# FFN up projections with the weights stationary, attention outputs scaled after the product, modulation sums at the FFNs' ends

## The chip, the core and the metric

The kernel runs on one core of one Trainium2 chip. The metric is the device time of one execution in microseconds (us). Matmuls run on TensorE (PE; its weight loads are listed as PEld), elementwise work on VectorE (DVE) and ScalarE (ACT), some on GpSimd (POOL); SyncE (SP) starts the weight transfers. Engines run on their own and meet at semaphores. TensorE writes to PSUM, which has eight banks of 512 fp32 columns here: acc0 to acc3, turn0, turn1, score0, score1.

## What is computed

256 tokens of width 1024 go through a block of two layers (unchanged here) and then through this one, of which the reference says:

```
a, g = jnp.split(h @ wi, 2, axis=-1)
return (a * jax.nn.silu(g)) @ wo                       # swiglu; D_FF = 2816
y = 0.5 * swiglu(modulate(x, mod, j), wi, wo)          # half_ffn_sublayer, then layer_norm(ALPHA*x + gate*y)
p = jax.nn.softmax(jnp.concatenate([s_win, s_ctx, sinks], axis=-1), axis=-1)
o = einsum(p[..., :SPAN], v_b) + einsum(p[..., SPAN:], vc)
mod_lat = (silu_c @ mod_w[i] + mod_b[i]).reshape(-1, N_MOD, D_MODEL)
```

Five FFNs run: FFN1 on x, FFN2 on the context, then attention, FFN3 and FFN4 on x, a Fourier mixer, FFN5 on x. Each modulation vector set (layer, j) must be there before the sublayer that uses it.

## The kernel before

**Products.** Every fp32 weight matrix is streamed in pieces of 128x1024. ACT rounds a piece to w_hi, DVE makes w_lo = raw - w_hi (split, L1038 and L1417); four slots hold split pieces, and ACT and DVE are up to four ahead of PE (a slot is free when PE has counted piece_done). Activations are kept the same way (xT_hi, xT_lo; features on partitions). product (L522) issues three fp32r matmuls with the activations stationary (128 features x 128 tokens) and 512 weight columns moving: L524, L525, L526.

**An FFN.** The up projection goes in 11 chunks of 256 hidden features (a and g, so 512 columns). project computes a chunk as two token tiles, 48 matmuls into two banks. ACT takes the silu of the g halves (L1274), DVE multiplies (L1872, hidden). Tokens are then on the partitions, but the down projection needs features there: one chunk later PE transposes hidden with four matmuls (turn_hidden, L842), ACT makes hT_hi (L1278) and DVE hT_lo (L1879). The first chunk stands ahead of a loop of five iterations with two chunks each. After the loop comes the last turn_hidden, and then the down projection: 22 pieces of 12 matmuls into acc0 to acc3. FFN3, FFN4 and FFN5 begin with project_first: the tokens 0 to 127 are turned (turn_tile, L561) and multiplied while the second tile's layer norm still runs. gate_rows (L830) ends the first chunk on PE.

**Modulation.** In four of the FFNs (FFN1 to FFN4) one modulation set of the future is computed on the side: POOL loads mod_w (L440), DVE sums eight scaled rows (mod_feature, L1536), and after each 512 columns PE adds over the partitions with four fp32 matmuls of one column (mod_sum, L632), which the profile lists as eight. That is one mod_sum in each loop iteration and one in the down projection.

**Attention.** Eight iterations u, each with two heads. PE: scores(u+1) (L934), values(u-1) (L963), turn_probs(u) (L947). DVE adds the band and takes maxima (L1972), ACT takes exp (L1322), DVE the inverse sums (L1984). POOL then multiplies the probabilities by them (L477, four instructions of 128x512 in each u), and PE transposes the result through three banks in turn; DVE and ACT move them out (L1989, L1330). ACT and DVE split the value products (L1333, L1996).

## Time and profile before

| what | us |
|---|---|
| median of 3 runs | 1750.22 |
| lowest, highest | 1747.34, 1750.8 |
| profiled execution, its own time | 1747.65 |
| its span, first to last instruction | 1745.9 |
| mean granted TensorE clock | 0.966 |

The profile is of one execution. A busy share says how much of the span an engine had an instruction under way. In the timeline a matmul's length runs past the start of the next one, so what a matmul costs in a stream is the spacing of the starts. A note in brackets is the idle time just before an instruction and what ended it.

### The profile page before, as it was taken

Reading aid. Unit: us, or ns where it says so; the run is one execution under the profiler, and the core shown is the slowest. Engines: PE = TensorE matmul, PEld = TensorE weight load, DVE = VectorE, ACT = ScalarE, POOL = GpSimd, SP = SyncE. Lnnn points to the kernel's source line nnn. Section 1 sums busy time; section 2 is a strip of 40 time slices with the busy share of each in tenths; the row PEclk is TensorE's granted clock in tenths of the full one; section 3 lists DMA queues with packets and bytes.
Section 4 is the critical chain, followed back from the end, with each engine's and each line's share of the span. In section 5 each row is a group of like instructions: output and inputs, shape, how many; then the busy total and the mean of one; then the engine's idle time right before and its main releaser. Section 6 shows DMA issues by size and latency. Waiting matters only on the chain.

```text
span 1745.9 us, 23849 instructions
## 1 busy us (share of the span) xinstructions
PE 1627.5 (93%) x7599; PEld 1313.8 (75%) x7599; DVE 1222.9 (70%) x1919; ACT 811.9 (47%) x1256; POOL 169.9 (10%) x207
## 2 busy tenths in 40 slices
PE   6989989899889999999998788999989998989997
PEld 6877768787778887788877357888778886678876
DVE  6877888787977774777667647777487765375545
ACT  5455445556354453444444545444354443254442
POOL 1100001100001110011000551110011100000000
PEclk9999989999989999999999889999999999999999
DMA  9763549642668875788555006887578863255541
GB/s 318 262 212 113 168 138 330 219 169 97 211 214 263 266 240 190 223 267 262 209 175 193 1 25 218 271 265 256 169 229 261 269 234 125 83 166 178 189 177 64
DMA packets 199330, 345.70 MB, mean 198 GB/s; under 512 B 10853, under 2 KB 127901, under 8 KB 198733
## 3 DMA queue, kind: packets, MB, share of 16 engines
q1 hardware_dynamic: 174668, 252.90, 43.5%
q0 software_dynamic: 24576, 91.73, 16.7%
q8 instruction: 46, 0.75, 0.2%
q14 instruction: 40, 0.32, 0.1%
...
## 4 chain that ended last, share of the span: by engine, by line
PE 83%; DVE 8%; issue 3%; ACT 3%; POOL 2%; DMA 0%; SPq 0%; DVEq 0%; ACTq 0%
PE acc L524 24%; PE acc L526 24%; PE acc L525 24%; POOL att_work L477 2%; DVE w_lo L1417 2%; PE score L632 2%; PE turn L842 1%; PE acc L743 1%; PE acc L995 1%; PE score L723 1%; DVE x L1517 1%; ACT turned L1102 1%; PE score L934 1%; ACT w_hi L1038 1%; PE score L830 1%
## 5 line engine op out<-in xcount | busy, mean ns | idle before, releaser
L1417 DVE TENSOR_TENSOR w_lo<-raw,w_hi 128x1024 fp32r<-128x1024 f32 (+1 forms) x490 | 585.4, 1200 | 309.3 <-ACT w_hi L1038 304.2
L1038 ACT ACTIVATE w_hi<-raw 128x1024 fp32r<-128x1024 f32 (+1 forms) x490 | 507.6, 1041 | 575.2 <-PE acc L526 574.8
L524 PE MATMUL acc<-w_hi,xT_hi 128*128 128x512 f32 (+1 forms) x1456 | 589.1, 405 | 33.2 <-DVE xT_lo L1464 12.4
L526 PE MATMUL acc<-w_hi,xT_lo 128*128 128x512 f32 (+1 forms) x1456 | 574.1, 394 | 0.0
L525 PE MATMUL acc<-w_lo,xT_hi 128*128 128x512 f32 (+1 forms) x1456 | 573.9, 394 | 0.0
L524 PEld LDWEIGHTS acc<-w_hi,xT_hi 128*128 128x128 f32 x1456 | 279.4, 192 | 95.7 <-issue 37.8
L526 PEld LDWEIGHTS acc<-w_hi,xT_lo 128*128 128x128 f32 x1456 | 278.6, 191 | 58.9
L525 PEld LDWEIGHTS acc<-w_lo,xT_hi 128*128 128x128 f32 x1456 | 279.9, 192 | 55.3 <-issue 1.2
L440 POOL DMA_DIRECT2D mod_raw<-in_mod_w x144 | 104.3, 724 | 999.1 <-DVE acc_lat L1536 957.7
L1536 DVE SCALAR_TENSOR_TENSOR acc_lat<-mod_raw,silu_c,acc_lat 128x512 f32<-128x512 f32 x252 | 187.8, 745 | 0.9 <-DMA mod_raw<-in_mod_w 0.9
L524 PE MATMUL acc<-w_hi,hT_hi 128*128 128x512 f32 x440 | 174.9, 397 | 0.7 <-DVE hT_lo L1879 0.3
L526 PE MATMUL acc<-w_hi,hT_lo 128*128 128x512 f32 x440 | 173.8, 395 | 0.0
L525 PE MATMUL acc<-w_lo,hT_hi 128*128 128x512 f32 x440 | 173.8, 395 | 0.0
L524 PEld LDWEIGHTS acc<-w_hi,hT_hi 128*128 128x128 f32 x440 | 82.6, 188 | 21.5 <-DVE hT_lo L1879 1.9
L526 PEld LDWEIGHTS acc<-w_hi,hT_lo 128*128 128x128 f32 x440 | 82.6, 188 | 20.0
L525 PEld LDWEIGHTS acc<-w_lo,hT_hi 128*128 128x128 f32 x440 | 82.6, 188 | 19.6
L1274 ACT ACTIVATE silu_g<-acc 128x256 f32<-128x256 f32 x110 | 36.3, 382 | 87.0 <-PE acc L526 87.0
L477 POOL TENSOR_SCALAR att_work<-att_work,att_inv 128x512 f32<-128x512 f32 x32 | 49.6, 1564 | 74.4 <-DVE att_inv L1984 74.4
L1872 DVE TENSOR_TENSOR hidden<-acc,silu_g 128x256 f32<-128x256 f32 x110 | 41.6, 420 | 15.5 <-ACT silu_g L1274 15.5
L1536 DVE SCALAR_TENSOR_TENSOR acc_ctx<-mod_raw,silu_c,acc_ctx 128x512 f32<-128x512 f32 x70 | 52.2, 746 | 0.0
L1879 DVE TENSOR_TENSOR hT_lo<-turn,hT_hi 128x512 f32 (+1 forms) x55 | 38.1, 692 | 9.6 <-ACT hT_hi L1278 3.4
L1179 ACT ACTIVATE work<-score,neg_max 128x256 f32<-128x256 f32 x64 | 29.7, 473 | 28.6 <-DVE neg_max L1637 28.6
...
## 6 DMA issues: line engine op xcount, KB each, us to landing
...
raw<-in_ffn_wo SPq DMA_DIRECT2D x110, 512.0 KB, 4.5
...
```

Source lines behind the costliest of these rows:

```text
L440: pool.dma_start(mod_raw[:, s, :, :], w_mod[l, :, 2 * i:2 * i + 2, at]).then_inc(mod_in[s], 16)
L477: m = nc.gpsimd.tensor_scalar(p, p, att_inv[:, h, t:t + 1], None, ALU.mult)
L524: nc.tensor.matmul(dst, xh, wh, start=start, stop=False)
L525: nc.tensor.matmul(dst, xh, wl, start=False, stop=False)
L526: return nc.tensor.matmul(dst, xl, wh, start=False, stop=stop)
L632: m = nc.tensor.matmul(dst[:, 4 * i + j:4 * i + j + 1], acc[:, 1, j * P:j * P + P], ones[:, 0:1], start=True, stop=True)
L1038: nc.scalar.activation(w_hi[:, i % SPLIT_SLOTS, 0:n], raw[:, s, i % 2 * PIECE:i % 2 * PIECE + n], ACT.Copy).then_inc(hi_ready, 1)
L1274: nc.scalar.activation(silu_g[:, half, t, :], bank[ACC[2 * half + t]][:, FC:2 * FC], ACT.Silu).then_inc(silu_done, 1)
L1417: nc.vector.tensor_tensor(w_lo[:, i % SPLIT_SLOTS, 0:n], raw[:, i // 2 % RAW_SLOTS, i % 2 * PIECE:i % 2 * PIECE + n], w_hi[:, i % SPLIT_SL ...
L1536: m = nc.vector.scalar_tensor_tensor(out=acc[:, 1 if k == KD - 1 else 0, :], in0=w, scalar=by, in1=acc[:, 0, :], op0=ALU.mult, op1=ALU.add)
L1872: nc.vector.tensor_tensor(hidden[:, half, t, :], bank[b][:, 0:FC], silu_g[:, half, t, :], ALU.mult).then_inc(moved[b], 1)
L1879: nc.vector.tensor_tensor(sl(hT_lo), bank[b][:], sl(hT_hi).bitcast(F32), ALU.subtract).then_inc(moved[b], 1)
```

## The change

- **Up projection.** up_product makes the weights stationary (128 x 128 features) and lets xT_hi or xT_lo move, so that hidden features come out on partitions. A chunk is 96 matmuls of 256 tokens; one bank holds a (two feature tiles), the other g. turn_hidden and its transposes go. ACT takes one silu of 512 columns, DVE one product of 512, ACT makes hT_hi from hidden and DVE hT_lo. One of a chunk's four splits now stands behind the silu.
- **First chunk by tile** (up_first: FFN3, FFN4, FFN5): the same matmuls with one token tile each, so 192 matmuls of 128 columns.
- **Down projection.** It starts with the column half 1 of the pieces 0 and 1 (banks acc2, acc3), then their half 0.
- **Modulation sums.** DVE leaves six sums in mod_kept; PE adds them over the partitions after the last down matmul (kept_sums). FFN1 and FFN2 do all 24 fp32 matmuls there; FFN3 and FFN4 do 8 there and 16 behind the next turn_tile. The sets (1,1) and (1,2) change places.
- **Attention.** The probabilities are transposed unscaled. PE spreads the inverse sums over a fifth transposed bank in each u, ACT moves it (move_scale), DVE multiplies the value product by it (scale_out), and POOL splits the result into xT_hi and xT_lo (two instructions of 128x256). The four probability banks and the scale go round the same three banks.

```diff
-            for h in range(AH):
-                pool.wait_ge(inv_ready, h + 1)
-                for t in range(NT):
-                    p = att_probs[:, h // 2 % 2, h % 2, t, :]
-                    m = nc.gpsimd.tensor_scalar(p, p, att_inv[:, h, t:t + 1], None, ALU.mult)
-                m.then_inc(norm_ready, 1)
+            for u in range(AH // 2):
+                pool.wait_ge(out_scaled, u + 1)
+                nc.gpsimd.tensor_copy(xT_hi[:, u, :], att_out[:, u % 2, :]).then_inc(out_hi, 1)
+                pool.wait_ge(out_hi, u + 1)
+                nc.gpsimd.tensor_tensor(xT_lo[:, u, :], att_out[:, u % 2, :], xT_hi[:, u, :].bitcast(F32), ALU.subtract).then_inc(out_split, 1)
...
-            def project_first(banks):
+            def up_first(banks, kept):
                 slots, after = [], [turn_tile(0)]
+                if kept:
+                    kept_sums(KEPT_EARLY, MOD_KEPT)
+                dst = [take(b) for b in banks]
                 for t in range(NT):
-                    dst = take(banks[t])
                     for i in range(4):
                         if t == 0:
                             if i == 2:
...
                         if i % 2 == 0:
                             b, landed_at = after[t][i // 2]
                             pe.wait_ge(moved[b], landed_at)
-                        s = slots[i]
-                        for kk in range(2):
-                            k = 2 * i + kk
-                            m = product(dst[:], xT_hi[:, k, t * P:t * P + P], xT_lo[:, k, t * P:t * P + P],
-                                        w_hi[:, s, kk * 512:kk * 512 + 512], w_lo[:, s, kk * 512:kk * 512 + 512],
-                                        k == 0, k == KD - 1)
+                        for k in (2 * i, 2 * i + 1):
+                            m = up_product(dst, slots[i], k, slice(t * P, t * P + P), t == 0 and k == 0)
...
+            def up_product(dst, s, k, tokens, first):
+                kk = k % 2 * 512
+                for h in range(2):
+                    for j in range(2):
+                        f = slice(kk + h * FC + j * P, kk + h * FC + j * P + P)
+                        d = dst[h][:, j * TOK + tokens.start:j * TOK + tokens.stop]
+                        nc.tensor.matmul(d, w_hi[:, s, f], xT_hi[:, k, tokens], start=first and j == 0, stop=False, skip_group_check=True)
+                        nc.tensor.matmul(d, w_lo[:, s, f], xT_hi[:, k, tokens], start=False, stop=False, skip_group_check=True)
+                        m = nc.tensor.matmul(d, w_hi[:, s, f], xT_lo[:, k, tokens], start=False, stop=k == KD - 1, skip_group_check=True)
...
+            def up_chunk(banks, after=None):
+                dst = [take(b) for b in banks]
+                for i in range(4):
+                    if after:
+                        b, landed_at = after[i]
+                        pe.wait_ge(moved[b], landed_at)
+                    s = piece()
+                    for k in (2 * i, 2 * i + 1):
+                        m = up_product(dst, s, k, slice(0, TOK), k == 0)
+                    m.then_inc(piece_done, 1)
...
+            def kept_sums(first, last):
+                if first == 0:
+                    pe.wait_ge(mod_step, c.next("mod", 8 * MOD_KEPT) + 2 * MOD_RING)
+                    take("score1")
+                for i in range(first, last):
+                    for j in range(4):
+                        m = nc.tensor.matmul(bank["score1"][:, 4 * i + j:4 * i + j + 1], mod_kept[:, i, j * P:j * P + P], ones[:, 0:1],
+                                             start=True, stop=True)
...
-            def ffn(after, mods, then=None):
-                def turn_hidden(half):
-                    landed(*ACC[2 * half:2 * half + 2])
...
-                    dst = take(b)
-                    for f in range(2):
-                        for t in range(NT):
-                            m = nc.tensor.transpose(dst[:, f * TOK + t * P:f * TOK + t * P + P],
-                                                    hidden[:, half, t, f * P:f * P + P], ident[:])
-                    m.then_inc(full[b], 1)
-                    return b
+            def ffn(after, mods, then=None, kept=False, by_tile=True):
                 if after:
-                    project(ACC[0:2], 4, after=after)
+                    up_chunk(ACC[0:2], after)
                 else:
-                    project_first(ACC[0:2])
+                    up_first(ACC[0:2], kept)
                 gate_rows()
...
                 with c.loop(pe, N_FC // 2, per):
-                    project(ACC[2:4], 4)
-                    turn_hidden(0)
-                    project(ACC[0:2], 4)
-                    turn_hidden(1)
-                    if mods:
-                        mod_sum(False)
-                last = turn_hidden(0)
...
+                    up_chunk(ACC[2:4])
+                    up_chunk(ACC[0:2])
+                pe.wait_ge(hidden_split, c.next("hidden", N_FC - 1))
+                dst = [None, None] + [take(b) for b in ACC[2:4]]
...
                         m = product(dst[2 * n + t][:], hT_hi[:, k, t * P:t * P + P], hT_lo[:, k, t * P:t * P + P],
                                     w_hi[:, s, n * 512:n * 512 + 512], w_lo[:, s, n * 512:n * 512 + 512], k == 0, k == KF - 1)
                     return m
-                for k in range(KF - 4):
+                slots = [piece() for _ in range(2)]
+                for k in range(2):
+                    for t in range(NT):
+                        down(k, slots[k], t, (1,))
+                dst[0:2] = [take(b) for b in ACC[0:2]]
+                for k in range(2):
+                    for t in range(NT):
+                        m = down(k, slots[k], t, (0,))
+                    m.then_inc(piece_done, 1)
+                for k in range(2, KF - 4):
                     if k == 4 and then:
                         after = then()
-                    if mods and k == KF // 2:
-                        mod_sum(False)
                     s = piece()
                     for t in range(NT):
                         m = down(k, s, t)
                     m.then_inc(piece_done, 1)
-                pe.wait_ge(moved[last], last_at)
+                pe.wait_ge(hidden_split, c.next("hidden"))
                 slots = []
                 for t in range(NT):
                     for i in range(4):
...
                             m.then_inc(piece_done, 1)
                     if t == 0:
                         m.then_inc(first_done, 1)
+                if mods:
+                    kept_sums(0, KEPT_EARLY if by_tile else MOD_KEPT)
...
-                        pe.wait_ge(norm_ready, c.next("norm"))
+                        pe.wait_ge(exps_ready, c.next("exps"))
...
+                    pe.wait_ge(inv_ready, c.next("inv", 2))
+                    b = att_turn(u, 4)
+                    dst = take(b)
+                    for t in range(NT):
+                        for i in range(2):
+                            m = nc.tensor.matmul(dst[i * AD:i * AD + AD, t * P:t * P + P], att_inv[:, 2 * u + i, t:t + 1].to_broadcast([P, AD]),
+                                                 ident[:], start=True, stop=True)
+                    m.then_inc(full[b], 1)
+                    turned_at[u].append((b, c.now(b) + 1))
...
-            after = ffn(turn_x(), True, turn_ctx_in)
-            after = ffn(after, True, turn_x)
+            after = ffn(turn_x(), True, turn_ctx_in, by_tile=False)
+            after = ffn(after, True, turn_x, by_tile=False)
             attention(after)
             ffn(None, True)
-            ffn(None, True)
+            ffn(None, True, kept=True)
...
-                def chunk(half, n=4):
+                def chunk(half, n=3):
                     split(n)
                     products(4)
-                    for t in range(NT):
-                        nc.scalar.activation(silu_g[:, half, t, :], bank[ACC[2 * half + t]][:, FC:2 * FC], ACT.Silu).then_inc(silu_done, 1)
-                def turn_hidden(k):
-                    src = filled(next_turn())
-                    nc.scalar.activation(hT_hi[:, k, :].rearrange("p k n -> p (k n)"), src[:], ACT.Copy).then_inc(turn_hi, 1)
-                chunk(0, 4 - early)
+                    b = ACC[2 * half + 1]
+                    nc.scalar.activation(silu_g[:], bank[b][:], ACT.Silu).then_inc(moved[b], 1)
+                    split()
+                def hidden_hi(half, k):
+                    act.wait_ge(hidden_ready, c.next("hidden"))
+                    nc.scalar.activation(hT_hi[:, k, :].rearrange("p k n -> p (k n)"), hidden[:], ACT.Copy).then_inc(moved[ACC[2 * half]], 1)
...
+                def move_scale(u):
+                    b = att_turn(u, 4)
+                    nc.scalar.activation(att_scale[:, u % 2, :], filled(b)[:, 0:TOK], ACT.Copy).then_inc(moved[b], 1)
...
+                def chunk(half, features=(), n=3, into=None):
                     for i in range(n):
                         split()
                         if features:
-                            mod_feature(features[i], False)
-                    for t in range(NT):
-                        b = ACC[2 * half + t]
-                        dve.wait_ge(silu_done, c.next("silu_done"))
-                        nc.vector.tensor_tensor(hidden[:, half, t, :], bank[b][:, 0:FC], silu_g[:, half, t, :], ALU.mult).then_inc(moved[b], 1)
-                def turn_hidden(k):
...
-                    c.next(b)
-                    dve.wait_ge(turn_hi, c.next("hi"))
...
-                    nc.vector.tensor_tensor(sl(hT_lo), bank[b][:], sl(hT_hi).bitcast(F32), ALU.subtract).then_inc(moved[b], 1)
-                chunk(0, n=4 - early)
...
+                            mod_feature(features[i], False, into)
+                    a, g = ACC[2 * half:2 * half + 2]
+                    dve.wait_ge(moved[g], c.next(g + " moved") + 1)
+                    nc.vector.tensor_tensor(hidden[:], bank[a][:], silu_g[:], ALU.mult).then_inc(hidden_ready, 1)
+                    split()
+                    if features:
+                        mod_feature(features[n], False, into)
+                def hidden_lo(half, k):
+                    a = ACC[2 * half]
+                    dve.wait_ge(moved[a], c.next(a + " moved") + 1)
...
+                    nc.vector.tensor_tensor(lo, hidden[:], hi.bitcast(F32), ALU.subtract).then_inc(hidden_split, 1)
...
+            def kept_store(l, j):
...
+                nc.vector.tensor_tensor(mod_lat[:, l, at], filled("score1")[:, 0:4 * MOD_KEPT], modb[:, l, at], ALU.add).then_inc(moved["score1"], 1)
...
+                def scale_out(u):
+                    if u > 1:
+                        dve.wait_ge(out_split, u - 1)
+                    nc.vector.tensor_tensor(att_out[:, u % 2, :], filled(ATT_OUT)[:, 0:TOK], att_scale[:, u % 2, :], ALU.mult).then_inc(out_scaled, 1)
...
-            ffn(x, x_ready, mod_lat[:, 0, :], 2, mods=(1, 2), end=by_tile, early=1)
+            ffn(x, x_ready, mod_lat[:, 0, :], 2, mods=(1, 1), end=by_tile, early=1)
```

PE, the end of FFN1's loop body and the start of the down projection; before:

```order
L525 MATMUL acc1<-w_lo,xT_hi 128x512
L526 MATMUL acc1<-w_hi,xT_lo 128x512
L513 REGISTER_ALU
L842 MATMUL turn1<-ident,hidden 128x128 x4
L628 REGISTER_ALU
L507 REGISTER_ALU
L632 MATMUL score1<-ones,acc_lat 128x1 x4
L108 REGISTER_ALU
L108 COMPARE_AND_BRANCH
L842 MATMUL turn0<-ident,hidden 128x128 x4
L524 MATMUL acc0<-w_hi,hT_hi 128x512
L525 MATMUL acc0<-w_lo,hT_hi 128x512
```

The same place after:

```order
L647 MATMUL acc1<-xT_hi,w_hi 128x256
L648 MATMUL acc1<-xT_hi,w_lo 128x256
L649 MATMUL acc1<-xT_lo,w_hi 128x256
L110 REGISTER_ALU
L110 COMPARE_AND_BRANCH
L537 MATMUL acc2<-w_hi,hT_hi 128x512
L538 MATMUL acc2<-w_lo,hT_hi 128x512
L539 MATMUL acc2<-w_hi,hT_lo 128x512
L537 MATMUL acc3<-w_hi,hT_hi 128x512
L538 MATMUL acc3<-w_lo,hT_hi 128x512
L539 MATMUL acc3<-w_hi,hT_lo 128x512
```

The transposes and the sum between the last up matmul and the first down matmul are gone, and the down projection begins in acc2.

PE, the start of FFN3: the first token tile is turned and the first matmuls of the first chunk follow; before:

```order
L561 MATMUL turn0<-ident,x 128x128 x4
L561 MATMUL turn1<-ident,x 128x128 x4
L524 MATMUL acc0<-w_hi,xT_hi 128x512
L525 MATMUL acc0<-w_lo,xT_hi 128x512
L526 MATMUL acc0<-w_hi,xT_lo 128x512
L524 MATMUL acc0<-w_hi,xT_hi 128x512
```

The same place after:

```order
L574 MATMUL turn0<-ident,x 128x128 x4
L574 MATMUL turn1<-ident,x 128x128 x4
L647 MATMUL acc0<-xT_hi,w_hi 128x128
L648 MATMUL acc0<-xT_hi,w_lo 128x128
L649 MATMUL acc0<-xT_lo,w_hi 128x128
L647 MATMUL acc0<-xT_hi,w_hi 128x128
L648 MATMUL acc0<-xT_hi,w_lo 128x128
```

Twelve matmuls of 512 columns for two pieces of one token tile become 48 of 128 columns; the second tile's turn (score0) stands behind them as before.

PE in the attention, from turn_probs(u) to scores(u+2), u = 0; before:

```order
L947 MATMUL turn0<-ident,att_work 128x128 x4
L947 MATMUL turn1<-ident,att_work 128x128 x4
L947 MATMUL acc3<-ident,att_work 128x128 x4
L947 MATMUL turn0<-ident,att_work 128x128 x4
L934 MATMUL score0<-kT,qT 128x512
L934 MATMUL acc0<-kT,qT 128x512
```

The same place after:

```order
L989 MATMUL turn0<-ident,att_work 128x128 x4
L989 MATMUL turn1<-ident,att_work 128x128 x4
L989 MATMUL acc3<-ident,att_work 128x128 x4
L989 MATMUL turn0<-ident,att_work 128x128 x4
L997 MATMUL turn1<-ident,att_inv 64x128 x4
L976 MATMUL score0<-kT,qT 128x512
L976 MATMUL acc0<-kT,qT 128x512
L976 MATMUL score1<-kT,qT 128x512
```

A fifth bank, the spread inverse sums (L997), stands behind the four of the probabilities.

## Rows read from the trace of the kernel before

**Rows 1.** The page: busy time of PE and others, and the chain by engine.

```profile
PE 1627.5 (93%) x7599; PEld 1313.8 (75%) x7599; DVE 1222.9 (70%) x1919; ACT 811.9 (47%) x1256; POOL 169.9 (10%) x207
...
PE 83%; DVE 8%; issue 3%; ACT 3%; POOL 2%; DMA 0%; SPq 0%; DVEq 0%; ACTq 0%
```

**Rows 2.** Windows of one loop iteration, FFN1 (with modulation) and FFN5 (without).

```profile
core 0: us, PE busy (x) PEld busy (x) DVE busy (x) ACT busy (x) POOL busy (x), PEclk, DMA share, GB/s
535.04:558.88 23.84, 23.84 (x114) 19.73 (x113) 17.81 (x24) 10.56 (x16) 3.13 (x5) 1.00 0.83 259
1593.08:1615.77 22.69, 22.69 (x105) 18.80 (x104) 12.70 (x14) 10.56 (x14) 0.00 (x0) 1.00 0.59 185
```

**Rows 3.** Timeline (start us, us, instruction), PE: loop start, first down matmul, FFN1 and FFN5.

```profile
511.02 0.79 PE L524 MATMUL acc<-w_hi,xT_hi 128*128 128x512 f32 x1
...
631.30 0.50 PE L524 MATMUL acc<-w_hi,hT_hi 128*128 128x512 f32 x1
...
1559.05 0.79 PE L524 MATMUL acc<-w_hi,xT_hi 128*128 128x512 f32 x1
...
1674.77 0.50 PE L524 MATMUL acc<-w_hi,hT_hi 128*128 128x512 f32 x1 [0.17 <-DVE hT_lo L1879]
```

**Rows 4.** Timeline, PE: fp32r streams, 23 matmuls of 256 and 43 of 512 columns.

```profile
95.72 0.28 PE L525 MATMUL acc<-w_lo,cT_hi 128*128 128x256 f32 x1
...
98.22 0.28 PE L526 MATMUL acc<-w_hi,cT_lo 128*128 128x256 f32 x1
...
714.35 0.39 PE L526 MATMUL acc<-w_hi,xT_lo 128*128 128x512 f32 x1
...
723.89 0.39 PE L526 MATMUL acc<-w_hi,xT_lo 128*128 128x512 f32 x1
```

**Rows 5.** Fp32 matmuls of 1 column (chain: start, us) and 128 columns (timeline).

```profile
51.60 1.68 PE score L632 x16
...
184.62 2.01 PE L743 MATMUL acc<-wide,work 128*128 128x128 f32 x16
```

**Rows 6.** Timeline, PE: the first chunk of FFN3.

```profile
1065.54 0.77 PE L524 MATMUL acc<-w_hi,xT_hi 128*128 128x512 f32 x1 [2.79 <-DVE xT_lo L1464]
...
1070.37 0.63 PE L526 MATMUL acc<-w_hi,xT_lo 128*128 128x512 f32 x1
1071.38 1.09 PE L561 MATMUL score<-ident,x 128*128 128x128 f32 x8 [0.38 <-DVE x L1517]
...
1080.53 1.88 PE L830 MATMUL score<-gate_diag,ones 128*128 128x512 f32 x4
```

**Rows 7.** Timeline, PE: the first work behind FFN1, FFN2 and FFN3.

```profile
698.92 0.76 PE L524 MATMUL acc<-w_hi,xT_hi 128*128 128x512 f32 x1 [3.11 <-DVE gated L1826]
...
900.68 0.76 PE L524 MATMUL acc<-w_hi,xT_hi 128*128 128x512 f32 x1 [3.11 <-DVE gated L1826]
...
1266.24 1.09 PE L561 MATMUL turn<-ident,x 128*128 128x128 f32 x8 [1.32 <-DVE x L1517]
```

**Rows 8.** Attention: window (columns as Rows 2), and timeline of PE and DVE.

```profile
962.60:1038.10 75.50, 57.18 (x320) 32.70 (x320) 42.60 (x135) 37.71 (x103) 49.60 (x32) 0.86 0.00 1
...
971.02 1.14 PE L947 MATMUL turn<-ident,att_work 128*128 128x128 f32 x8 [2.78 <-POOL att_work L477]
...
979.27 1.08 PE L963 MATMUL acc<-ctx_x,qkv 128*64 128x256 f32 x8
...
984.88 0.69 PE L934 MATMUL score<-kT,qT 64*128 64x512 f32 x1
...
989.44 0.23 DVE L1978 TENSOR_SCALAR att_neg<-att_max,neg_sink 128x2 f32<-128x2 f32 x1
...
1036.28 1.08 PE L963 MATMUL acc<-ctx_x,qkv 128*64 128x256 f32 x8 [0.92 <-ACT ctx_x L1330]
```

**Rows 9.** Groups by line (last numbers: busy us, mean ns), from the page and by form.

```profile
L1417 DVE TENSOR_TENSOR w_lo<-raw,w_hi 128x1024 fp32r<-128x1024 f32 (+1 forms) x490 | 585.4, 1200 | 309.3 <-ACT w_hi L1038 304.2
L1038 ACT ACTIVATE w_hi<-raw 128x1024 fp32r<-128x1024 f32 (+1 forms) x490 | 507.6, 1041 | 575.2 <-PE acc L526 574.8
...
L1989 DVE COPY ctx_x<-turn 128x512 f32<-128x512 f32 x11 | 7.6, 688 | 6.7 <-PE turn L947 6.6
```

151 lines of the change are left out of this document (76 added, 75 removed).

## The prediction, made before the changed kernel was run

> **What bounds the kernel now.** I read the page's busy times and the chain of waits first. PE is busy 93% of the span and is 83% of the chain; DVE is 8% of it [rows 1]. So a change counts by what it takes from or gives to PE's sequence, and off PE only where PE stands and waits. Then I took windows of one FFN loop iteration: PE is busy in all of it, 23.84 us with modulation and 22.69 without, while DVE does 17.81 and ACT 10.56 [rows 2]. The reader is to see that PE never waits in the loop, and that the two windows differ by 1.15 us, the price of one mod_sum in PE's sequence. The timeline of PE at the joints gives the rest: what stands between loop start and first down matmul, how the first chunk by tile runs, how long PE idles behind an FFN, and who holds the attention.
>
> **What a matmul costs.** In a stream, 256 columns of fp32r are spaced (98.22 - 95.72) / 22 = 0.1136 us and 512 columns (723.89 - 714.35) / 42 = 0.2271 us [rows 4]. So 96 matmuls of 256 take 10.9 us and 48 of 512 take 10.9 us: exchanging the operands is free in the loop, and twice as many weight loads still hide behind 256 columns. A full iteration of 96 x 0.2271 = 21.8 us leaves 22.69 - 21.80 = 0.89 us for two turn_hidden.
>
> The Trainium skill speaks against this: "Perfetto Trace Analysis", section "Identifying the Most-Contended Engine", judges TensorE's headroom by the busy share of its weight loads. Taken alone it would double the 18.80 us of an iteration without modulation to 37.6 us, above 21.8, and add some 395 us over the 25 iterations. The 256-column row, where loads already come every 0.1136 us, contradicts that, so I give this no chance.
>
> **Part 1, up loop and start of the down projection.** FFN1 runs from 511.02 to 631.30, 120.3 us, for ten chunks [rows 3]; FFN2, FFN3 and FFN4 are within 0.3 us of that. After: 10 x 10.9 = 109.0 us, plus some 0.2 us that the first matmul behind gate_rows takes longer, 109.2. That is -11.1 us in each of four FFNs, -44.4. FFN5 has no sums: 1674.77 - 1559.05 = 115.7, so -6.5 us. The mod_sum in the middle of the down projection goes in four FFNs: 4 x -1.15 = -4.6 us. Together **-55.5 us**.
> What hides the new hand-over: PE needs acc0 again 12 half products, 2.7 us, after the last up matmul. ACT by then must do silu (not over 1.04 us, a split of 1024 columns), one split (1.04) and hT_hi, DVE one product of 512 columns between them (0.69, as L1989) [rows 9]: 1.04 + 1.04 + 0.6 = 2.7 us, so nearly even; without that cover it would cost up to 1 us per FFN. Behind the silu stands one split on each engine; its piece is needed two pieces (5.4 us) later, so PE doesn't wait for it. DVE has 17.81 of 21.8 us in an iteration, ACT 10.56.
> DMA moves as much in less time: share 0.83 x 23.84 / 21.8 = 0.91, 283 GB/s [rows 2]. I take it as enough; if it isn't, see the third rival.
>
> **Part 2, the first chunk by tile.** This is what the change costs, and the trace has no fp32r matmul under 256 columns. Bounds: nothing beyond the columns (128 at half of 0.1136, 0.057 us, so no loss); and the fp32 rate, where 16 instructions of 128 columns take (2.01 - 0.28) / 15 = 0.115 us each, two to a matmul, 0.23 us [rows 5]. I choose between them by the fp32 matmuls of one column: 16 in 1.68 us, 0.105 us each, though they stream nothing [rows 5]. With one column moving, what is left is the weight load, so I take 0.105 us for any matmul with fresh weights.
> FFN3 today: first matmul 1065.54, the matmuls ahead of the second turn_tile are spaced 0.43 us (half clock: the last of the twelve starts at 1070.37), and the turn waits until 1071.38 for the second tile's layer norm [rows 6]. So 5.8 us of time are there for these two pieces anyway. After: 48 matmuls; 24 in 5.1 us at half clock (0.21 each), 24 at 0.105, 7.6 us: 1.8 late. The other two pieces of the first tile: 48 x 0.105 = 5.0 against 12 x 0.227 = 2.7, 2.3 more. The second tile: 96 x 0.105 = 10.1 against 5.4, 4.7 more. Sum 8.8; three FFNs: **+26 us**.
> The Trainium skill bears on the choice. "TensorE: Matmul & The Clock Gate", section "LDWEIGHTS (loading the stationary operand)", has the load take its columns divided by 1.2 GHz; the row of 0.105 us agrees. The same page, section "Back-to-back issue gap", reports about 81 ns for sustained pairs at 128 columns. By that this part would be an estimated +14 us and the total 12 us lower; no row here shows such a spacing.
>
> **Part 3, the sums at the ends.** 24 fp32 matmuls are 48 instructions, 48 x 0.105 = 5.0 us. Behind FFN1 and FFN2 PE idles 3.1 us for a bank today [rows 7]: +1.9 us each. Behind FFN3 and FFN4 there are 16 instructions, 1.7 us, in an idle time of 1.32: +0.4 each. The remaining 32, 3.4 us, stand behind the turn where PE waits 2.79 or more for xT_lo [rows 6]: +0.5 at most once, since the attention's end has none. Together **+5 us**, from 0 (if the next chunk then starts at full clock; today its first matmuls are spaced 0.43) to +8.
>
> **Part 4, attention.** The stretch of 75.5 us has 49.6 us of POOL in 32 instructions, 1.55 each, 6.2 in every u, at a clock of 0.86 [rows 8]. values(0) starts at 979.27 and values(7) at 1036.28, 8.14 us for each u. Afterwards the first turn_probs need not wait for POOL (idle 2.78 before 971.02), which brings values(0) some 4 us forward. Then what is late next is the ring of three banks: the fourth probability bank of a u takes the first one again, and DVE moves that only after both maxima. From scores (984.88) to the end of those (989.44 + 0.23) are 4.8 us; then scale_out (0.4), a move (0.69, rows 9), the fourth transposes (0.5), the spread sums (8 instructions at 0.115, 0.9): 7.4 us, say 7.5 for each u. 8 x 0.6 = 5 us. Sum **-9 us**; from 0 (no gain if the fifth use of the ring costs what POOL did) to -16 (PE's own work). values(u) also waits for scale_out(u-1), queued on DVE behind two maxima; scores(u+1) cover it. POOL's two instructions of 256 columns in each u (1.6 us by its 1.55 for 512) end before the output product of the fourth piece.
>
> **Sum.** -55.5 + 26 + 5 - 9 = -33.5 us. The profiled execution's own time is 1747.65 (its span 1745.9), so 1714.2; the median lies 2.6 above it: **1716 us**, give or take 9.
>
> **Rivals.**
> - *Narrow fp32r runs at the fp32 rate* (the slower side). At 0.23 us in the three first chunks: 7.8 + 8.4 + 16.7 = 33 us for each instead of 8.8, so 1716 - 26 + 99 = 1789. It decides against the change from 0.16 us on, where the three chunks eat the 33 us. For it: fp32 at 128 columns does cost 0.23. Against: the stream of fp32r halves exactly from 512 to 256 columns [rows 4], with no sign of a second regime. 16%.
> - *Weight loads hide at 128 columns too.* Part 2 is then about 0: 1690. The 0.105 us of the one-column matmuls would be something of fp32 alone. 12%.
> - *Transfers hold the loop.* If more than 259 GB/s doesn't come, an iteration stays at up to 23.84 us in the four FFNs with modulation, 20 x 2.0 = 41 us back at most, 1757; half of it is 1736. DVE would then wait for mod_raw. Against: at a share of 0.83 the engines have room today [rows 2]. 12%.
> - Forecast as summed, 1705 to 1727: 60%.
>
> **How the numbers follow.** The range takes in the forecast, the second rival and the nearer half of the third: 1688 to 1742, which leaves out the fp32 rate (16%) and some 3% beyond the ends. Within 0.2% of before (3.5 us, about what a measurement of this kernel can tell from no change) lies only a corner of the third rival or a milder form of the first: 3%. Slower 16%, faster 81%.
>
> **What would show it.** Loop iteration 21.8 us in FFN1 and FFN5 alike, with no transposes in it (right), or near 23 with waits for mod_raw (third rival). Spacing of the 128-column matmuls in FFN3's first chunk: 0.105, 0.057 or 0.23 us; the stretch from its first matmul to gate_rows 24 us instead of 15. Behind FFN1 the next chunk starts 5 us after the last down matmul instead of 3.1. values(u) spaced 7.5 us, attention about 66 us. I am wrong if the stretch of the first chunks grows by over 15 us, or if PE has idle time inside the loop.

## The result, and the profile after the change

The changed kernel takes 1779.04 us (median of 4 runs, 1776.73 to 1781.66) against 1748.78 us for the kernel before on the same chip (4 runs). The ratio is 1.0176, 95% interval 1.0157 to 1.0195: slower by 1.8%, where 1716 us had been predicted. The profiled execution has a span of 1776.5 us, 30.6 more than before, and it is the one read below.

The page: PE and its weight loads, PE's granted clock in 40 slices, and the chain by engine.

```profile
PE 1688.3 (95%) x10371; PEld 1494.9 (84%) x10371; DVE 1200.4 (68%) x1844; ACT 798.0 (45%) x1201; POOL 129.9 (7%) x191
...
PEclk9999989999989998999998989999899998859999
...
PE 86%; DVE 7%; issue 3%; ACT 2%; DMA 1%; SPq 0%; DVEq 0%; ACTq 0%; POOLq 0%
```

PE is still the bound, busy for 61 us more than in [rows 1]. The second 8 and the 5 near the end of the clock's row belong to a stretch at half clock, 1542.4 to 1590.2 us, that the kernel before didn't have. The windows show it: an up loop iteration of FFN1 and one of FFN5, then the first chunks of FFN3, FFN4 and FFN5, from their first matmul to gate_rows.

```profile
core 0: us, PE busy (x) PEld busy (x) DVE busy (x) ACT busy (x) POOL busy (x), PEclk, DMA share, GB/s
550.00:573.04 23.04, 23.04 (x195) 23.04 (x194) 16.88 (x21) 10.11 (x13) 2.89 (x4) 1.00 0.86 281
1590.43:1613.47 23.04, 23.04 (x195) 23.04 (x194) 9.79 (x10) 8.72 (x10) 0.00 (x0) 1.00 0.52 159
1048.26:1076.72 28.46, 28.46 (x201) 28.46 (x201) 13.19 (x22) 7.51 (x14) 3.98 (x6) 0.77 0.60 199
1263.43:1291.83 28.40, 28.40 (x202) 28.40 (x202) 11.61 (x21) 5.03 (x10) 2.55 (x4) 0.78 0.46 162
1544.27:1586.89 42.62, 42.62 (x201) 42.62 (x201) 13.19 (x22) 7.51 (x14) 1.05 (x2) 0.50 0.31 99
```

Three more windows: the sums behind FFN1, the end of its down projection ahead of them, and the sums behind FFN2:

```profile
690.14:698.07 7.93, 7.93 (x50) 7.93 (x48) 7.86 (x13) 3.47 (x5) 0.00 (x0) 0.65 0.04 7
686.00:690.14 4.14, 4.14 (x19) 3.33 (x18) 2.90 (x8) 3.62 (x6) 0.00 (x0) 1.00 0.05 19
891.98:897.14 5.16, 5.16 (x48) 5.16 (x47) 5.09 (x10) 0.86 (x1) 0.00 (x0) 1.00 0.00 0
```

The first two windows show that an iteration takes 23.04 us with and without modulation (192 x 0.120), and that the weight loads are busy in all of it. The first chunks took 15.0 us before [rows 6]; now they take 28.5, 28.4 and 42.6, and the last ran at a granted clock of 0.50 from end to end although PE never stood still. The joints, in PE's timeline (start us, us, instruction):

```profile
509.87 1.88 PE L881 MATMUL score<-gate_diag,ones 128*128 128x512 f32 x4
...
626.78 0.40 PE L537 MATMUL acc<-w_hi,hT_hi 128*128 128x512 f32 x1
...
690.14 8.07 PE L682 MATMUL score<-ones,mod_kept 128*128 128x1 f32 x48
698.07 0.56 PE L647 MATMUL acc<-xT_hi,w_hi 128*128 128x256 f32 x1
...
959.16 0.66 PE L976 MATMUL score<-kT,qT 64*128 64x512 f32 x1 [0.83 <-issue]
...
1020.92 0.50 PE L537 MATMUL acc<-w_hi,xT_hi 128*128 128x512 f32 x1
...
1060.79 0.41 PE L647 MATMUL acc<-xT_hi,w_hi 128*128 128x128 f32 x1
...
1061.31 0.28 PE L647 MATMUL acc<-xT_hi,w_hi 128*128 128x128 f32 x1
1061.42 0.28 PE L648 MATMUL acc<-xT_hi,w_lo 128*128 128x128 f32 x1
...
1255.27 1.84 PE L682 MATMUL score<-ones,mod_kept 128*128 128x1 f32 x16
1256.98 1.07 PE L574 MATMUL turn<-ident,x 128*128 128x128 f32 x8
1257.88 5.69 PE L682 MATMUL score<-ones,mod_kept 128*128 128x1 f32 x32
1263.43 0.45 PE L647 MATMUL acc<-xT_hi,w_hi 128*128 128x128 f32 x1
```

With these the 30.6 us come apart nearly without rest. The parts are those of the prediction; before and after are PE's own times.

| part | stretch | measured | predicted |
|---|---|---|---|
| 1 | gate_rows to first down matmul, FFN1 to FFN4: 121.6 to 116.9 (FFN4 121.3) | -18.4 | -44.4 |
| 1 | the same in FFN5: 117.0 to 118.6 | +1.6 | -6.5 |
| 1 | first to last down matmul, without mod_sum: 1.0 less in each of FFN1 to FFN4, 0.1 in FFN5 | -4.1 | -4.6 |
| 2 | first chunks: 15.0 to 28.5, 15.0 to 28.4, 15.1 to 42.6 | +54.4 | +26 |
| 3 | sums at the ends (behind FFN1 alone +5.8, FFN2 +2.0, FFN3 and FFN4 +3.1) | +10.9 | +5 |
| 4 | first scores to output projection: 75.5 to 61.8 | -13.7 | -9 |
| | sum | +30.7 | -33.5 |

Parts 1 and 2 miss by 35 and 28 us, part 3 by 6; part 4 was better than said. The four questions for the chip follow from this: what the clock does in the first chunk, why 256 columns cost 0.120 and not 0.1136 us, whether parts 3 and 4 are worth by themselves what the table says, and what is left when only the good parts are kept.

### The profile page after: what moved, and what is told of

It is laid out like the page before. It is cut to its first block, busy times and chain, and to the rows that moved or that the text cites. A ratio compares the mean times of both kernels' runs of the same rounds, so it can differ in the third digit from the quotient of the medians.

```text
span 1776.5 us, 29013 instructions
## 1 busy us (share of the span) xinstructions
PE 1688.3 (95%) x10371; PEld 1494.9 (84%) x10371; DVE 1200.4 (68%) x1844; ACT 798.0 (45%) x1201; POOL 129.9 (7%) x191
## 4 chain that ended last, share of the span: by engine, by line
PE 86%; DVE 7%; issue 3%; ACT 2%; DMA 1%; SPq 0%; DVEq 0%; ACTq 0%; POOLq 0%
PE acc L647 13%; PE acc L649 13%; PE acc L648 13%; PE acc L537 12%; PE acc L539 12%; PE acc L538 12%; DVE w_lo L1465 2%; PE score L682 2%; PE acc L794 1%; PE acc L1045 1%; PE score L976 1%; DMA mod_raw<-in_mod_w 1%; PE score L774 1%; DVE att_work L2025 1%; PE score L881 1%
## 5 line engine op out<-in xcount | busy, mean ns | idle before, releaser
L647 PE MATMUL acc<-xT_hi,w_hi 128*128 128x256 f32 (+1 forms) x1856 | 542.5, 292 | 7.0 <-DVE xT_lo L1512 7.0
L648 PE MATMUL acc<-xT_hi,w_lo 128*128 128x256 f32 (+1 forms) x1856 | 539.5, 291 | 0.0
L649 PE MATMUL acc<-xT_lo,w_hi 128*128 128x256 f32 (+1 forms) x1856 | 539.3, 291 | 0.0
L647 PEld LDWEIGHTS acc<-xT_hi,w_hi 128*128 128x128 f32 x1856 | 372.8, 201 | 9.3 <-issue 9.3
L648 PEld LDWEIGHTS acc<-xT_hi,w_lo 128*128 128x128 f32 x1856 | 372.5, 201 | 1.4 <-issue 1.4
L649 PEld LDWEIGHTS acc<-xT_lo,w_hi 128*128 128x128 f32 x1856 | 372.2, 201 | 0.0
L537 PE MATMUL acc<-w_hi,xT_hi 128*128 128x512 f32 (+1 forms) x576 | 234.6, 407 | 16.0 <-DVE xT_lo L1500 6.9
L538 PE MATMUL acc<-w_lo,xT_hi 128*128 128x512 f32 (+1 forms) x576 | 227.8, 395 | 0.0
L539 PE MATMUL acc<-w_hi,xT_lo 128*128 128x512 f32 (+1 forms) x576 | 227.7, 395 | 0.0
L538 PEld LDWEIGHTS acc<-w_lo,xT_hi 128*128 128x128 f32 x576 | 111.7, 194 | 21.0
```

The costliest lines, as they stand in the source:

```text
L537: nc.tensor.matmul(dst, xh, wh, start=start, stop=False)
L538: nc.tensor.matmul(dst, xh, wl, start=False, stop=False)
L539: return nc.tensor.matmul(dst, xl, wh, start=False, stop=stop)
L647: nc.tensor.matmul(d, w_hi[:, s, f], xT_hi[:, k, tokens], start=first and j == 0, stop=False, skip_group_check=True)
L648: nc.tensor.matmul(d, w_lo[:, s, f], xT_hi[:, k, tokens], start=False, stop=False, skip_group_check=True)
L649: m = nc.tensor.matmul(d, w_hi[:, s, f], xT_lo[:, k, tokens], start=False, stop=k == KD - 1, skip_group_check=True)
```

## The experiments

### The first chunk: width and clock

**wide_first.** The chunk waits for both tiles and runs 96 matmuls of 256 columns.

```diff
-                for t in range(NT):
-                    for i in range(4):
...
-                        for k in (2 * i, 2 * i + 1):
-                            m = up_product(dst, slots[i], k, slice(t * P, t * P + P), t == 0 and k == 0)
+                after.append(turn_tile(1))
+                for i in range(4):
...
+                    for k in (2 * i, 2 * i + 1):
+                        m = up_product(dst, s, k, slice(0, TOK), k == 0)
```

> The changed kernel with one edit: the first chunk of FFN3, FFN4 and FFN5 waits for both token tiles and then runs with 256 columns, 96 matmuls instead of 192 of 128 columns. Theory A (the narrow matmuls are the loss: 0.112 us each at the full clock, 0.213 at the half clock, which they keep): 96 matmuls take 11.5 us at the full clock, up to 20.5 at the half one, after a start 12 to 15 us later. In FFN3 from 1048.3 the first chunk then ends after some 14 + 12 to 20 us = 26 to 34 instead of 28.6; in FFN5 14 + 12 to 20 = 26 to 34 instead of 42.8. Total 1779 - 9 to -16 if the clock rises early, 1763 to 1770. Rival B (the half clock stays through the chunk of FFN5 whatever the width): FFN5 gains 8 us, FFN3 and FFN4 lose 5 each, total 1779 to 1782.

Measured: 1744.82 us (10 runs), ratio to before 0.9985 [0.9968, 1.0001]: 34 us less than the changed kernel, more than either theory gave. The window of its first chunk in FFN3 shows why:

```profile
1054.00:1057.40 3.40, 3.35 (x16) 3.38 (x17) 2.79 (x10) 0.12 (x1) 0.06 (x1) 0.50 1.02 354
1057.60:1067.00 9.40, 9.40 (x80) 9.40 (x80) 2.45 (x2) 2.12 (x2) 0.00 (x0) 1.00 0.82 284
```

With 256 columns the clock came back 3.5 us after the first matmul, in FFN4 after 3.6 and in FFN5 after 3.1 us. I had expected the half clock to last for up to all of the chunk. The narrow chunk held it for 12.9 us in FFN3, 12.8 in FFN4 and 42.6 us in FFN5. So either the narrow stream can't raise the clock, or it lowers it by itself.

**warm_narrow** tells these apart. The narrow chunk stays, and PE is kept busy ahead of it (TN is 448 columns).

```diff
                 dst = [take(b) for b in banks]
+                for _ in range(3):
+                    nc.tensor.matmul(dst[0][:, 0:TN], ident[:], tables[:].rearrange("p t n -> p (t n)")[:, 0:TN], start=True, stop=True)
```

> The changed kernel with one addition: in the idle time between the first turn_tile and the first chunk of FFN3, FFN4 and FFN5, PE runs three fp32 matmuls over 448 columns of a constant, into the bank that the chunk then starts afresh. The narrow first chunk itself stays. In the changed kernel it ran at a granted clock of 0.50 for 13 us in FFN3 and FFN4 and for all of its 43 us in FFN5. Theory A (the stream of narrow matmuls cannot raise the clock, yet keeps what it has): with PE busy ahead of it the chunk of FFN5 runs at the full clock, 192 x 0.112 = 21.5 us instead of 41, and in FFN3 and FFN4 the first half takes 5.4 instead of 10.3 us (then it waits for the second tile, so 0 to 5 us each). Total 1779 - 20 - 0 to 10 = 1749 to 1759. Rival B (the narrow stream lets the clock fall whatever it starts with, or three matmuls are too few): the chunk of FFN5 stays near 43 us, total 1776 to 1783.

Measured: 1748.37 us, 0.9995 [0.9979, 1.0011] of before, 31 us less than the changed kernel. Theory A gave 1749 to 1759, just above it. A window of FFN5, from the second turn_tile to gate_rows:

```profile
1541.95:1558.90 16.95, 16.95 (x152) 16.95 (x153) 7.43 (x15) 5.02 (x10) 1.05 (x2) 1.00 0.47 146
```

The clock is 1.00 in all of it. The same narrow stream keeps the full clock that it is given. From the first turn_tile to gate_rows FFN3 now takes 26.7 us against 32.3 in the changed kernel and 18.9 before. The 7.8 us over before are the cost of the narrow width itself; the rest was the clock. The prediction's 8.8 had 24 matmuls at half clock in it; without them its sum gives 7.0.

**cut_first** asks whether this is a matter of weights being loaded. It is the kernel before with each 512-column matmul of the first chunk cut in four.

```diff
-                            m = product(dst[:], ..., w_hi[:, s, kk * 512:kk * 512 + 512], ...)
+                            for c0 in range(0, 512, P):
+                                m = product(dst[:, c0:c0 + P], ..., w_hi[:, s, kk * 512 + c0:kk * 512 + c0 + P], ...)
```

> The kernel before with one edit: in the first chunk of FFN3, FFN4 and FFN5 each matmul of 512 columns is cut into four of 128, with activations loaded as before; 192 narrow matmuls, as many as in the changed kernel. Theory A (the width alone does it, whatever is loaded): first matmul to gate_rows 28.6 us in FFN3 and FFN4 as in the changed kernel, 20.5 to 43 in FFN5 by when the clock rises: total 1749 + 13.6 + 13.6 + 8 to 28 = 1784 to 1804. Rival B (loading weights instead of activations does it, or the modulation sums ahead of the chunk): the clock rises after some 5 us as before, each chunk costs 8 us more, total 1749 + 24 = 1773.

Measured: 1817.47 us, 1.0399 [1.038, 1.0418]: above even theory A. In FFN3 the clock came back within the chunk as in the changed kernel, in FFN4 and FFN5 not before gate_rows (first turn_tile to gate_rows 32.2, 47.6 and 46.5 us). A window of FFN5's chunk:

```profile
1596.00:1628.00 32.00, 32.00 (x152) 32.00 (x152) 7.58 (x15) 6.08 (x11) 0.00 (x0) 0.50 0.22 73
```

So the width does it, whichever operand is loaded. When the clock comes back varies. PE's second turn_tile in the changed kernel, FFN3 and FFN5:

```profile
1058.53 1.93 PE L574 MATMUL score<-ident,x 128*128 128x128 f32 x8
...
1554.55 1.93 PE L574 MATMUL score<-ident,x 128*128 128x128 f32 x8
```

These eight fp32 instructions interrupt the narrow stream. The clock came back inside a narrow chunk five times in the traces (FFN3 and FFN4 of the changed kernel and of shared_w, FFN3 here), each time 0.4 to 0.7 us behind the end of the second turn_tile. Four chunks with the same turn_tile stayed at the half clock to their end (FFN5 of the changed kernel and of shared_w, FFN4 and FFN5 here). There it came back 3.3 to 3.6 us after gate_rows, of 512 columns, had begun. So no trace shows a return behind narrow fp32r matmuls alone; whether it is turn_tile that brings the clock back was not tested by itself. One run in four of shared_w (below) took 1762 instead of 1777 us at a mean clock of 0.964 instead of 0.955.

### The spacing of 0.120 us in the loops

The prediction took 0.1136 us from 23 matmuls of 256 columns with cT loaded [rows 4]. I went through what differs between these and the loop.

**shared_w** puts the two matmuls with the same weights in a row.

```diff
-  matmul(d, w_hi[:, s, f], xT_hi[:, k, tokens], ...)
-  matmul(d, w_lo[:, s, f], xT_hi[:, k, tokens], ...)
+  matmul(d, w_lo[:, s, f], xT_hi[:, k, tokens], ...)
+  matmul(d, w_hi[:, s, f], xT_hi[:, k, tokens], ...)
   matmul(d, w_hi[:, s, f], xT_lo[:, k, tokens], ...)
```

> The changed kernel with one edit: each group of three matmuls of the up projection runs w_lo.x_hi, w_hi.x_hi, w_hi.x_lo instead of w_hi.x_hi, w_lo.x_hi, w_hi.x_lo, so that the two with the same weights stand in a row. Theory A (the 0.120 us between 256-column matmuls, where the row of before had 0.1136, is there because every matmul has other weights than the one ahead, while in the row of before two of three share them): spacing 0.1136, an iteration of the loop 21.8 us instead of 23.04, total 1779 - 32 = 1747 us. Rival B (a load costs the same whatever stood there): spacing stays 0.120, total 1779 within 3 us.

Measured: 1777.32 us, spacing 0.120. Theory A falls.

**cut_256** exchanges the operands back: the kernel before, with the loop's matmuls cut in two.

```diff
-                            m = product(dst[t][:, 0:n], ...)
+                            for c0 in range(0, n, n // cut):
+                                m = product(dst[t][:, c0:c0 + n // cut], ...)
...
-                    project(ACC[2:4], 4)
+                    project(ACC[2:4], 4, cut=2)
```

> The kernel before with one edit: in the up loop of the FFNs every matmul of 512 columns is cut into two of 256 columns, each with its own load of the activations; as many loads as in the changed kernel, but activations are what stays. Theory A (it is the weights as the loaded side that cost 0.120): spacing 0.1136, iteration without modulation 22.7 us as before, total 1749. Rival B (it is the surroundings, two engines and the transfers busy beside a load every 256 columns, that cost it): spacing 0.120, iteration 22.7 + 1.2 = 23.9, total 1749 + 30 = 1779.

Measured (one run): 1777.9 us, spacing 0.1199. First, second and last of 61 of its matmuls:

```profile
576.77 0.28 PE L526 MATMUL acc<-w_hi,xT_lo 128*128 128x256 f32 x1
576.89 0.28 PE L524 MATMUL acc<-w_hi,xT_hi 128*128 128x256 f32 x1
...
583.96 0.28 PE L526 MATMUL acc<-w_hi,xT_lo 128*128 128x256 f32 x1
```

Which operand is loaded plays no part; with either, halving a matmul costs some 5.5% more per column in the FFNs. FFN5 after the change has a DVE busy 9.8 us an iteration and a DMA share of 0.52, FFN1 16.9 and 0.86, both at exactly 0.120, so the engines beside PE aren't it either.

**wide_six**, **wide_alt** and **wide_bank** change where results go: six in a row to one place; two banks in turn after each matmul; another bank after every three. The lines are shortened.

```diff
wide_six:   for h, j, k in ((h, j, k) for h in range(2) for j in range(2) for k in (2 * i, 2 * i + 1)):
wide_alt:   for j in range(2): for w, xt in ((w_hi, xT_hi), (w_lo, xT_hi), (w_hi, xT_lo)): for h in range(2):
wide_bank:  for j in range(2): for h in range(2):
```

> The kernel with the first chunk of 256 columns (1745 us), with one edit in every chunk of the up projection: the loop over the two features of a piece is the innermost, so that six matmuls in a row add into the same 256 columns of a bank instead of three. Theory A (the 0.120 us in the loops, where the row of before with 256 columns had 0.1136 and six to a place, comes from changing the place of the result every three matmuls): spacing 0.1136, an iteration 21.8 instead of 23.04 us, total 1745 - 31 = 1714. Rival B (the place plays no part): 0.120 stays, total 1745 within 3.

> The kernel with the first chunk of 256 columns (1745 us), with the matmuls of the up projection in another order: two places of the result in different banks take turns, so that no matmul adds to what the one ahead of it wrote. Theory A (0.120 us instead of 0.1136 because a matmul must read back what the one before has just written, 256 columns ago): spacing 0.1136, an iteration 21.8 us, total 1745 - 31 = 1714. Rival B (not so): spacing 0.120, total 1742 to 1748.

> The same kernel, with the bank changed after every three matmuls, as the row of before with 0.1136 us has it; the changed kernel stays in a bank for six. Theory A (the change of bank is what made that row fast): 0.1136, total 1714. Rival B: 0.120, total 1742 to 1748; then order, operand and bank are all excluded and the difference between the two spacings stays open.

Measured: 1744.5, 1743.71 and 1739.96 us (one run each for the last two), all with 116.9 us from gate_rows to the first down matmul. Three more explanations fall.

**burst**, **burst_acc**, **burst_x** and **burst_c** work on the fast stream itself and make it four or five times as long. What stands behind the colons is told in short.

```diff
-   m = product(dst[...], cT_hi[:, 2, ...], cT_lo[:, 2, ...], w_hi[:, s, 0:256], w_lo[:, s, 0:256], True, True)
burst:      + for _ in range(4): the same product, True, True
burst_acc:  + for r in range(4): the same product, r == 0, r == 3
burst_x:    + for r in range(4): product(..., xT_hi[:, 2 * r, ...], xT_lo[:, 2 * r, ...], ..., True, True), then the old one
burst_c:    + for k in (0, 1, 0, 1, 2): product(..., cT_hi[:, k, ...], cT_lo[:, k, ...], ..., True, True)
```

> The kernel before with the stream of 24 matmuls of 256 columns, which had the 0.1136 us, made four times as long: each of its products is run four times into the same place, always started afresh (96 matmuls, twice in the program). Theory A (only a short stream runs at 0.1136): the spacing goes to 0.120 after the first 24 or so. Rival B (the kind of product decides, not the length): 0.1136 for all 96, total 1749 + 2 x 8.2 = 1765.

> As the stream made four times as long, but the twelve matmuls of a place add up instead of being started afresh every three (so this product comes out four times too large). Theory C (adding to what is there is what costs, and in the short stream one in three starts afresh): spacing 0.120. Otherwise as the long stream that starts afresh.

> The same place in the kernel before: ahead of each product of the short stream stand four more with the FFNs' activations as weights (each started afresh and overwritten, 120 matmuls in all). Theory D (the activations xT, which lie in another place of memory than cT, are what costs 0.120): those four products at 0.120, the fifth at 0.1136. Otherwise all at the value of the long stream.

> The kernel before; ahead of each product of the stream of 24 stand four more with the other two features of cT as weights (120 matmuls in all, each product started afresh, the last one overwrites). In the stream made four times as long (0.1134 us) every load brought the same few weights again; with xT's features in turn it was 0.1195. Theory D (the tile xT lies where it costs, cT does not): 0.1134 for all. Rival E (loading the same weights again and again is what was fast, other weights each time cost 0.120 whatever the tile): 0.1195 as with xT.

Measured (one run each, 1768.71, 1761.86, 1774.06 and 1769.71 us). Second and last matmul of the stream, first of burst (94 spacings), then of burst_x (118), then of burst_c (118):

```profile
95.99 0.28 PE L525 MATMUL acc<-w_lo,cT_hi 128*128 128x256 f32 x1
...
106.66 0.28 PE L526 MATMUL acc<-w_hi,cT_lo 128*128 128x256 f32 x1
```

```profile
95.78 0.28 PE L525 MATMUL acc<-w_lo,xT_hi 128*128 128x256 f32 x1
...
109.88 0.28 PE L526 MATMUL acc<-w_hi,cT_lo 128*128 128x256 f32 x1
```

```profile
96.78 0.28 PE L525 MATMUL acc<-w_lo,cT_hi 128*128 128x256 f32 x1
...
110.17 0.28 PE L526 MATMUL acc<-w_hi,cT_lo 128*128 128x256 f32 x1
```

That is 0.1135, 0.1195 and 0.1135 us; burst_acc had 0.1134. Length, adding up and new weights each time play no part. The stream at the same place in the program costs 0.0060 us more for each matmul when four of five products take their weights from xT. Theory D came out in half: the products with xT took 0.120 us a matmul, but those with cT that stand between them took 0.119, not 0.1136. So the tiles that a matmul itself reads don't settle what it costs. xT and cT differ in where they lie in each partition: in the kernel before w_hi, w_lo and xT begin 128 bytes behind a multiple of 512, cT begins 192 behind one, and cT lies farther from w_hi (172 KB against 41).

**pad** and **pad_w** move the tiles, on top of wide_bank. A pad moves every tile allocated behind it as well: pad shifts hT and cT by 64 bytes too, while in pad_w only w_hi, w_lo and x begin at another remainder of 512 bytes.

```diff
pad:    +        pad = sb("pad", [P, 16])          (ahead of xT_hi: xT at 192)
pad_w:  +        pad_w = sb("pad_w", [P, 16])      (ahead of w_hi: w_hi, w_lo at 192)
pad_w:  +        pad_x = sb("pad_x", [P, 112])     (ahead of xT_hi: xT at 128)
```

> The kernel with the first chunk of 256 columns and the bank changed every three matmuls (1740 us), with a pad of 64 bytes in each partition ahead of xT, so that xT no longer begins on the same remainder of 512 bytes as w_hi and w_lo do; cT in the fast stream differs from them by just that. Theory D1 (loads and moving columns meet in the same part of the memory when the remainders are the same): spacing 0.1136, total 1740 - 31 = 1709. Rival (the remainder plays no part): 0.120, total 1738 to 1748.

> The same kernel as the one with the pad ahead of xT (256-column first chunk, bank changed every three matmuls), but with 64 bytes ahead of w_hi and 448 ahead of xT: now the loaded weights begin 64 bytes behind the remainder (of 512 bytes) of the moving xT, as the loaded cT does against the moving weights in the fast stream; with the pad ahead of xT alone it was the other way round and gave 0.1178 us (loop and gate_rows to first down matmul 114.8 us instead of 116.9). Theory D2 (the direction matters: what is loaded must lie ahead): spacing 0.1134, gate_rows to first down matmul 110.7 us, total 1742 - 5 x 4.1 = 1722. Rival F (the regions of the memory in which the tiles lie decide the rest; cT lies some 170 KB behind w_hi, xT some 40): spacing 0.117 to 0.120, total 1740 to 1750.

Measured: pad 1742.7 us (one run), spacing 0.1178 in all five FFNs, a gain of 2.1 us in each loop; theory D1 had hoped for more. The total is no lower than wide_bank's 1739.96: with xT loaded, the 512-column matmuls of the projections went from 0.2272 to 0.2333. pad_w: 1729.27 us (5 runs), 0.9893 [0.9871, 0.9915], short of theory D2's 1722. Its profile is of the fastest of the five, 1719.13 us, at a mean clock of 0.965 where the others have 0.954 to 0.964. In it, second and last matmul of the up loop of FFN1 and of FFN5 (958 spacings each):

```profile
508.26 0.28 PE L647 MATMUL acc<-xT_hi,w_lo 128*128 128x256 f32 x1
...
616.85 0.28 PE L648 MATMUL acc<-xT_lo,w_hi 128*128 128x256 f32 x1
...
1534.88 0.28 PE L647 MATMUL acc<-xT_hi,w_lo 128*128 128x256 f32 x1
...
1647.71 0.28 PE L648 MATMUL acc<-xT_lo,w_hi 128*128 128x256 f32 x1
```

FFN1 ran at 0.1133, FFN2 to FFN5 at 0.1178. The 512-column matmuls moved too: in the down projections (hT loaded, at 448 bytes behind a multiple of 512) they are spaced 0.2333 us before and after the change and 0.2268 in pad_w, while the projections with xT went from 0.2272 to 0.2290. So where the tiles lie moves the spacing by some 1 to 6%, shown by the pads, which change nothing else. That it is the place of the loaded and the moving tile against each other was argued, not shown. The rule stays open: the offset of 64 bytes that cT has gives 0.1133 in one FFN of pad_w and 0.1178 in four, with every tile at the same place in all five, so the place isn't all of it. And the offset 0 is the worst for 256 columns and near the best for 512.

### Parts 3 and 4 alone, and together

**att_alone** and **sums_alone** are the kernel before with one part of the change; **att_and_sums** has both and leaves the up projections as they were.

```diff
att_alone:   turn_probs, values, scale_out, move_scale and POOL's split of the outputs as in the change
sums_alone:  mod_kept, kept_sums and kept_store as in the change; project_first(banks, kept)
```

> The kernel before with the change to the attention alone (outputs scaled by the inverse of the row sum after the value product, split on POOL; a ring of five uses). Theory A (the gain of the attention in the changed kernel is its own: from the first scores to the output projection 61.8 us instead of 75.5): values(u) spaced 6.9 us, total 1749 - 13 = 1736. Rival B (part of it comes from the earlier layer norms or transfers of the rest of the change, or is given back in FFN3's start): 1740 to 1745.

> The kernel before with the change to the modulation sums alone: no mod_sum in the loop or the down projection, the six sums of an FFN at its end, 16 of 48 instructions there and 32 behind the next turn_tile where an FFN ends by tile. Theory A (its price is what the changed kernel shows at the ends, 4.8 us behind FFN1, 2.1 behind FFN2, some 1.7 at four other places): 24 x 1.15 = 27.6 us less in the loops and down projections, 11 to 14 more at the ends: 1749 - 15 = 1734. Rival B (the loops without it are held by the transfers of modulation weights, which have 22.7 us instead of 23.84 an iteration): DVE waits for mod_raw, iterations over 23 us, 1742 or more.

> The kernel before with both the attention's change and the modulation sums at the ends; the up projections as before (results with tokens on partitions, first chunk by tile with 512 columns). If the two add: 1736 - 15 = 1721. Rival (they share an idle time, or the transfers hold the loop): 1730.

Measured: att_alone 1736.44 us, 0.9931 [0.9915, 0.9948], scores to output projection 61.7 us: the attention's gain is its own (theory A). sums_alone 1741.05 us, 0.9949 [0.9927, 0.9971], a gain of 8 where 15 was expected. Its loops got faster by 4.2 to 4.6 us in each of four FFNs, with no wait of PE, so the transfers didn't hold them; but FFN1 as a whole, gate_rows to gate_rows, takes 201.6 us against 201.8, since the sums at its end give all of it back. The gain is in FFN3 and FFN4 (5.4 and 2.1 us). att_and_sums: 1721.89 us, **0.9844 [0.9804, 0.9883]**. This beats both kernels: 1.6% faster than before, 3% faster than the change. Apart the two gave 12 and 8 us, together 27. The four runs spread from 1712.62 to 1729.46 us, so that they do more than add isn't shown. Part of the spread lies in the sums: in this profile, the fastest run, the 48 instructions behind FFN1 and FFN2 took 5.5 and 5.8 us, in that of sums_alone 7.8 and 8.0, where the clock fell earlier.

**best_busy** adds the three busy matmuls to it.

```diff
                 for t in range(NT):
                     dst = take(banks[t])
+                    for _ in range(3 if t == 0 else 0):
+                        nc.tensor.matmul(dst[:, 0:TN], ident[:], tables[...][:, 0:TN], start=True, stop=True)
```

> The kernel with the attention's change and the sums at the ends (1722 us), with PE kept busy between turn_tile and the first chunk by three fp32 matmuls over 448 columns of a constant, as in the narrow kernel where it gave 31 us. There the 256 to 512 column chunks kept the half clock only for 3 to 5 us, and behind that PE waits for the second tile anyway: a gain of 0 to 1 us in each of three FFNs, total 1719 to 1722. Rival (the busy start also shortens the way to the second tile or the rest of the chunk): 1712 to 1718; or the extra matmuls delay the first chunk: 1723 to 1727.

Measured: 1728.1 us, 0.9871 [0.9837, 0.9905], no gain; the interval overlaps that of att_and_sums, so a loss isn't shown by the times either. From the first turn_tile to gate_rows the three FFNs take 20.4, 21.9 and 20.5 us instead of 18.9, 19.7 and 19.2: ahead of these wide chunks the extra matmuls cost more than they give back.

## Why the prediction was wrong

- **What bounds the kernel.** Right: PE, and no idle time of PE in the loops. DVE waits 19 us for mod_raw in all, which costs PE nothing; the third rival (transfers hold the loop) didn't happen, at 281 GB/s; in pad_w's FFN1 an iteration took 21.76 us at 289 GB/s, the pace that the prediction asked for.
- **What a matmul costs: the first step that failed.** "256 columns ... 0.1136", so "exchanging the operands is free". The row was read rightly and carried to where it doesn't hold. In the loops 256 columns cost 0.120: 960 x 0.0064 = 6.1 us in each FFN, 31 us in all. cut_256 shows that the price is that of halving the matmuls with these tiles, and the pads that the place of the tiles is in it; the rest of the cause is open. The prediction's sentence that the first pair of rows shows "no sign of a second regime" rested on one stream in one place.
- **The page on weight loads.** The Trainium skill ("Perfetto Trace Analysis", section "Identifying the Most-Contended Engine") would have doubled the loads' busy time to 37.6 us an iteration. It became 23.04, the whole window. Giving that no chance was right. The loads' busy share couldn't have warned of the 0.120 either: in the stream at 0.1136 us [rows 4] they are busy in all of the 2.50 us as well.
- **Part 1.** Predicted -55.5, measured -20.9. Of the 35 us, 31 are the spacing and 1.4 FFN5's gate_rows at half clock (its loop starts 2.7 us behind it instead of 1.3); a mod_sum in the down projection had cost 1.0 us, not 1.15. The hand-over to the down projection was right: the first down matmul follows the last up matmul in 0.12 us.
- **Part 2: the second step that failed.** The full-clock cost was nearly right: 0.1117 us against the chosen 0.105, 7.8 us a chunk against the 7.0 that the sum gives without its half clock. The Trainium skill's 81 ns (section "Back-to-back issue gap" of "TensorE: Matmul & The Clock Gate") was seen in no run. What failed is "24 in 5.1 us at half clock": the half clock for the first 24 of the narrow matmuls only. That was read from a chunk of 512-column matmuls [rows 6], in which the clock came back in 5 us. In the narrow chunks it came back after 12.8 and 12.9 us, and in FFN5 not at all. That is 31 us in the three chunks, shown by warm_narrow, which takes them away and leaves the width; the prediction had 2.5 us of half clock in each.
- **The first rival** (fp32 rate, 0.23 us, 1789) gave nearly the right total with the wrong mechanism. Its 0.23 and the measured 0.213 at half clock lie close by chance, and one look at the granted clock tells them apart. Its total also stands on a loop at 0.1136 us that didn't come.
- **Part 3.** +5 predicted, +10.9 measured. Behind FFN1 the 48 one-column instructions took 7.9 us, 0.165 each, not 0.105 [rows 5]: the clock fell 2.4 us into them (0.65 over the stretch, 1.00 ahead of it), and the next chunk then starts at half clock, as before. Behind FFN2 it fell only at their end, and the same 48 took 5.3 us. Over all traces they took 5.3 to 8.0 us; the price of 0.105 is one of the full clock.
- **Part 4.** -9 predicted, -13.7 measured. values(u) came every 6.9 us instead of the 7.5 that the ring of banks was thought to need (its terms add up to 7.3, not 7.4; which of them was too long isn't shown); the last two, without scores beside them, came faster still. att_alone gives 12 us on its own.
- The text named what would prove it wrong, a first chunk longer by over 15 us. FFN5's grew by 27.5, those of FFN3 and FFN4 by 13.5 and 13.4.
